# A two-block layer on one Trainium2 core: where the layer norm's sums stand in the order, who squares the MLP's tiles, and at what pace the mixers run

## What is computed

```python
# first block: 12 heads are mixed (4 gated linear attention, 4 HGRN, 4 cross attention)
proj = einsum('bsd,de->bse', rms_norm(x, norm_w), w_in)
gla_o  = merge_heads(rms_norm(chunked_gated_linear_attention(gq, gk, gv, gla_log_a), gla_norm_w))
hgrn_o = merge_heads(rms_norm(chunked_gated_linear_attention(hq, hgrn_k, hi, hgrn_log_f), hgrn_norm_w))
x = x + einsum('bse,ed->bsd', concatenate([gla_o, hgrn_o, xo]) * silu(gate), w_out)

# second block: conformer convolution, then the MLP
u = h @ w_pw1 + b_pw1
a, gate = split(u, 2)
u = dwconv(a * sigmoid(gate), w_dw) + b_dw          # 31 taps per channel
u = silu(layer_norm(u, ln_g, ln_b))                  # mean, then sum of squares, over the channels
xl = xl + g1 * (u @ w_pw2 + b_pw2)
xl = xl + g2 * (square(relu(modulate(rms_norm(xl)) @ w1)) @ w2)      # 4096 hidden
return rms_norm(xl, final_g)
```

## Time and profile before

| | |
|---|---|
| median of 3 runs | 2219.56 us (2217.82 to 2226.28) |
| the profiled execution | 2225.21 us, span 2223.4 us |
| TensorE's granted clock over the span | 0.961 of full speed |
| PE busy | 2099.5 us, 94% |
| DVE, ACT, POOL busy | 50%, 33%, 37% |
| products L1228 with WH, with WL | 951.7 us (x2976), 572.9 us (x1488) |

### The profile page before, as it was taken

The page is one execution under the profiler, slowest core; times in us unless marked ns, Lnnn a source line. Parts: engine busy times, 40 slices in busy tenths (PEclk is TensorE's granted clock), DMA queues, the critical chain, the costliest instruction groups (busy, mean ns, idle before and its releaser), DMA issues. The chain is left out here.

```text
span 2223.4 us, 26465 instructions
## 1 busy us (share of the span) xinstructions
PE 2099.5 (94%) x10318; PEld 1750.1 (79%) x10318; DVE 1120.0 (50%) x1941; ACT 723.1 (33%) x1251; POOL 825.6 (37%) x493
## 2 busy tenths in 40 slices
PE   7899999898998889999989988799999999999997
PEld 5778988787887678888878777667878888888886
DVE  5353455356463245455569968887425222222225
ACT  2312322211036622231456547442423222212211
POOL 7352122212111354443338857553344442222220
PEclk9999999999899999999999979899899999999998
DMA  4111011111001476776335422122223331111112
GB/s 161 58 57 52 16 58 57 39 34 34 29 29 39 144 292 227 236 242 212 114 135 190 180 79 80 59 74 76 76 77 101 98 95 57 59 55 48 48 48 76
DMA packets 68845, 213.55 MB, mean 96 GB/s; under 512 B 7648, under 2 KB 8032, under 8 KB 68592
## 3 DMA queue, kind: packets, MB, share of 16 engines
q1 hardware_dynamic: 54896, 186.69, 24.8%
q10 hardware_dynamic: 13824, 25.17, 3.6%
HBM read 182.47 MB, written 29.36 MB: 95 GB/s over the span
## 5 line engine op out<-in xcount | busy, mean ns | idle before, releaser
L1228 PE MATMUL B<-HB,WH 128*128 128x512 f32 x2976 | 951.7, 408 | 25.2 <-ACT WH L1625 11.0
L2457 POOL TENSOR_TENSOR WL<-RAW,WH 128x1024 fp32r<-128x1024 f32 x201 | 487.5, 2428 | 627.6 <-ACT WH L1625 623.5
L1228 PEld LDWEIGHTS B<-HB,WH 128*128 128x128 f32 x2976 | 562.2, 194 | 148.9 <-issue 28.0
L1228 PE MATMUL B<-HB,WL 128*128 128x512 f32 x1488 | 572.9, 399 | 7.6 <-POOL WL L2457 7.6
L1228 PEld LDWEIGHTS B<-HB,WL 128*128 128x128 f32 x1488 | 287.2, 193 | 73.0 <-POOL WL L2457 10.6
L1625 ACT ACTIVATE WH<-RAW 128x1024 fp32r<-128x1024 f32 x160 | 168.5, 1055 | 435.3 <-DMA RAW<-wall 421.6
L1939 DVE SCALAR_TENSOR_TENSOR B<-UP,vec,B 128x512 f32<-128x512 f32 x308 | 207.5, 746 | 0.0
L1939 DVE SCALAR_TENSOR_TENSOR RES<-B,modv,RES 128x512 f32<-128x512 f32 x144 | 104.5, 746 | 193.4 <-PE B L1411 167.6
L1411 PE MATMUL B<-HIDH,WH 128*128 128x512 f32 x512 | 188.4, 401 | 3.9 <-DVE RES L1939 2.0
L2434 POOL TENSOR_TENSOR small<-small 128x4 f32<-128x4 f32 (+2 forms) x36 | 36.7, 1019 | 397.1 <-DVE small L1942 397.0
L1411 PE MATMUL B<-HIDH,WL 128*128 128x512 f32 x512 | 183.6, 392 | 0.0
(11 more groups left out here) (242 smaller groups left out, 2733.2 us busy)
## 6 DMA issues: line engine op xcount, KB each, us to landing
RAW<-wall SPq DMA_DIRECT2D x201, 512.0 KB, 3.6
MODRAW<-wmod ACTq DMA_DIRECT2D x96, 256.0 KB, 4.3
WH<-parts SPq DMA_DIRECT2D x32, 512.0 KB, 3.2
WL<-parts SPq DMA_DIRECT2D x32, 512.0 KB, 4.2
RES<-xT SPq DMA_DIRECT2D x16, 512.0 KB, 8.9
oscr<-OT SPq DMA_DIRECT2D x32, 256.0 KB, 2.0
OI<-oscr SPq DMA_DIRECT2D x16, 512.0 KB, 5.2
parts<-WH SPq DMA_DIRECT2D x16, 512.0 KB, 5.2
```

The lines of the kernel that those rows point to most:

```text
L1228: i = pe.matmul(bank, a[:, ks], hb(part, k, h), start=k == 0 and n == 0, stop=k == 7 and n == 2)
L2457: po.tensor_tensor(lo, raw, hi.bitcast(F32), ALU.subtract).then_inc(sig[f"w_lo{q % NW}"], 1)
```

## The change

1. **The layer norm's sums.** `LATE` becomes 8 us for the first half and 22 for the second. Each `ysum` waits until 5 (first half) or 12 us (second half) after its `ysub` on the plan's clock, singly and no longer in pairs; `ln_row` until 5 us after `ln_r`. When all DVE channels of a half are out, the tap lanes' lead falls from 2.5 to -2.5 us, until the norm is written.
2. **The square.** ScalarE does Relu, Square (into the PSUM bank) and the high part; VectorE does only the low part. Two taps are put between in VectorE's order, where there are some.
3. **The MLP's order.** The first half's group 3 comes before the second half's pw2, and the hidden tiles 16 to 19 of the first half run beside the second half's norm. Their weights are loaded once per half, four units of 512 KB more.
4. **The mixers' pace.** Each step of a mixer has its own price in credit (0.6 to 1.5, before 1.0 for all). At the end of a q product only the mixer's own list is run out; what finishes a mixer stays for later products.
5. **The last levels.** The matmuls of levels 4 and 5 take 112 and 96 weight columns, not 128, and the masked copies as many partitions.

```diff
-LATE = 8.0
+LATE, LATE_SQ, LATE_ROW = (8.0, 22.0), (5.0, 12.0), 5.0
...
             elif h:
-                mlp[h] += [("w1", (g + 1) * GT + i, 2) for i in range(GT)]
+                mlp[h] += [("w1", (g + 1) * GT + i, h) for i in range(GT)]
...
         while credit[0] >= 1.0 and (bg or bg2):
-            credit[0] -= 1.0
-            step()
+            credit[0] -= step()
...
+    def mixed_up_to(n):
+        while len(bg) > n:
+            step_in(bg)
...
-            project(("gq", h), "q_out", h, lambda: drain(1))
+            project(("gq", h), "q_out", h, lambda: mixed_up_to(1))
...
-            project(("hq", n - 4), "q_out", n, lambda: drain(1 if i == 0 else 0))
+            project(("hq", n - 4), "q_out", n, lambda: mixed_up_to(1 - i))
...
+        if all((i, h) in co_done or i in BY_POOL[h] for i in range(8)):
+            ahead[0] = -2.5
...
     def normed(h):
         take(S, "ysum", h)
+        made = []
         for f in range(8):
             piece("ysub", f, h)
             piece("ysq", f, h)
-            if f % 4 == 3:
-                yield
+            made.append(now["dve"])
         for f in range(8):
+            yield from until(made[f] + LATE_SQ[h])
             piece("ysum", f, h)
             if f % 2:
                 yield
         piece("ln_r", h)
-        for _ in range(8):
-            yield
+        yield from until(now["pe"] + LATE_ROW)
...
+    def squared(i, h):
+        piece("hid", i, h)
+        for _ in range(2):
+            if lanes["dve"]:
+                lane_step("dve")
+        piece("hid_lo", i, h)
...
+    half_group(AHEAD_GROUPS - 1, 0)
...
     second_product(1)
     bg.append(before_mlp(1))
-    half_group(AHEAD_GROUPS - 1, 0)
+    for i in range(GT):
+        hidden(AHEAD_GROUPS * GT + i, 0)
     drain()
...
-                m = 64 if l == 6 else 128
+                m = 128 - (1 << l) if l > 3 else 128
...
                 ac.activation(RL[:, :], BANKS[b], ACT.Relu).then_inc(sig["hid_relu"], 1)
+                w.wait_ge(sig["hid_relu"], n)
+                ac.activation(BANKS[b], RL[:, :], ACT.Square).then_inc(sig["hid_sq"], 1)
...
-                stt(BANKS[b], BANKS[b], 0.0, RL[:, :], ALU.max, ALU.mult).then_inc(sig["hid_sq"], 1)
```

More of the change, by code:

```diff
@@ L37 @@
 COST = {"dve": {"glu": 0.7, "tap": 0.67, "taps_end": 0.7, "ysub": 0.7, "ln_r": 0.8, "z_mul": 0.7, "z_lo": 1.2, "pre": 0.75,
-                "pw2": 0.75, "sq_add": 0.65, "sq_add3": 0.7, "m1_mul": 0.66, "m1_lo": 0.66, "m2_mul": 0.75, "m2_lo": 1.5, "hid": 1.4,
+                "pw2": 0.75, "sq_add": 0.65, "sq_add3": 0.7, "m1_mul": 0.66, "m1_lo": 0.66, "m2_mul": 0.75, "m2_lo": 1.5, "hid_lo": 0.7,
                 "w2_out": 0.75},
@@ L86, in unit_plan @@
             elif h:
-                mlp[h] += [("w1", (g + 1) * GT + i, 2) for i in range(GT)]
+                mlp[h] += [("w1", (g + 1) * GT + i, h) for i in range(GT)]
             mlp[h] += [("w2", g, j, h) for j in range(4)]
-    plan += [("pw2", f, 0) for f in range(8)] + mlp[0][:-4]
-    plan += [("pw2", f, 1) for f in range(8)] + mlp[0][-4:] + mlp[1]
+    plan += [("pw2", f, 0) for f in range(8)] + mlp[0]
+    plan += [("pw2", f, 1) for f in range(8)] + [("w1", AHEAD_GROUPS * GT + i, 0) for i in range(GT)] + mlp[1]
     for g in range(AHEAD_GROUPS, HG):
@@ L258, in step @@
         turn[0] += 1
-        step_in(bg2 if (bg2 and turn[0] % 2) or not bg else bg)
+        return step_in(bg2 if (bg2 and turn[0] % 2) or not bg else bg)
     def step_in(lane):
         try:
-            next(lane[0])
+            return next(lane[0]) or 1.0
         except StopIteration:
             lane.pop(0)
+            return 1.0
+    def mixed_up_to(n):
+        while len(bg) > n:
+            step_in(bg)
     def drain(upto=0):
@@ L370, in finish @@
         for _ in range(LATER[0]):
-            yield
+            yield 0.6
         piece("scale", n, hh)
         for _ in range(LATER[1]):
-            yield
+            yield 0.6
         for f in range(tiles):
@@ L499, in make_plan @@
     for h in range(4):
-        project(("xq", h), "q_out", 8 + h, lambda: drain(1))
+        project(("xq", h), "q_out", 8 + h, lambda: mixed_up_to(1))
         bg.append(cross(8 + h))
-    while len(bg) > 1:
-        step()
+    mixed_up_to(1)
     ring = [G]
@@ L721, in means @@
         while left:
-            ready = [f for f in left if (f, h) in co_done and (now["pe"] > co_done[f, h] + LATE or hurry[0])]
+            ready = [f for f in left if (f, h) in co_done and (now["pe"] > co_done[f, h] + LATE[h] or hurry[0])]
             if ready:
@@ L728, in means, with until @@
             yield
+    def until(us):
+        while now["pe"] < us and not hurry[0]:
+            yield
     def normed(h):
         take(S, "ysum", h)
+        made = []
         for f in range(8):
@@ L757, in conv_norm @@
         yield from normed(h)
+        ahead[0] = AHEAD
     hi_by[0] = "act"
@@ L847, in hidden @@
         for h in halves:
-            piece("hid", i, h)
+            squared(i, h)
     def half_group(g, h):
@@ L888, in make_plan @@
         for i in range(GT):
-            hidden((g + 1) * GT + i, *((1,) if g + 1 < AHEAD_GROUPS else (0, 1)))
+            hidden((g + 1) * GT + i, 1)
         half_group(g, 1)
```

22 lines of the change are left out of this document (10 added, 12 removed).

## The result

| | before | with the change |
|---|---|---|
| median of 4 runs | 2218.69 us (2210.6 to 2226.28) | 2192.28 us (2187.83 to 2194.9) |
| profiled execution, span | 2225.21 us, 2223.4 us | 2192.47 us, 2190.7 us |
| mean granted clock | 0.961 | 0.971 |

The ratio is 0.9879, 95% interval 0.9841 to 0.9918: 26 us faster, where 40 were forecast. To see where they came from I cut both traces at five matmuls that stand in each kernel: the first of the gate (GLR,gupt), the last of the values (WL,HB, into B), the first with w_out (MXH,WH), the first mean (CO,ones), and the first MLP product with w2 (HIDH,WL). The last column ends at the last norm's first broadcast (FIN,ones). Each number is the time between two such matmuls, in us.

What follows compares the result with a forecast made beforehand. The prediction took TensorE, busy 94% of the span, as the bound, with gains only in its waits and half-clock stretches. Terms 13 + 6 + 3 + 1 + 9 + 7 + 1 = 40 us took 2219.6 to 2180, range 2152 to 2204.

Steps and rivals of the forecast that it cites:

- Mixers, the transposes: Transposes at mixer drains: waits for OSB and the half clock behind them go; 13 us, bounds 0 and 14.8.
- Levels of head 6: Head 6's mixer levels: a product step before each wait cuts idle time and half clock; 6 us, bounds 0 and 10.7.
- Mixers, the rest: Two more mixer transposes stand behind more products, less a cost for bare levels; 3 us, bounds -1.3 and 4.3.
- The rival that the mixers' gain is given back: Mixers: VectorE paces levels and chunks, waits return at later buffer uses, 22 us lost; 2202 us, chance 0.13.
- Narrower levels: Mixers' last levels: fewer weight columns shorten weight loads; 1 us, bounds 0 and 3.6.
- First half's layer norm: First half's sums of squares: the 7.81 us wait goes, most half clock stays; 9 us, bounds -1 and 23.3.
- Second half and hidden tiles: Second half: waits for mean and squares go, HIDL waits halve, 7 us; half clock at the sums, 1 us.
- The square: MLP hidden tiles: 64 squares moved to ScalarE run beside products, relieving VectorE; 0 us on the path.
- The rival that ScalarE becomes the path: MLP: each hidden tile waits for its square, 40 us come back; 2220 us, no change, chance 0.03.
- Extra units: MLP weights: four more loads and splits are covered by idle DMA, ScalarE and GpSimd; 0 us.
- The clock stayed up: Rival: full clock in both halves' sums, adding 14 us in the first and 11 in the second; 2155, chance 0.12.
- The slower rival: Mixer drains: longer runs without products lower the clock in each of six, 8.35 us apiece; 2235 us, chance 0.04.

Runs made afterwards that it cites:

- experiment 1: The kernel before, with only the change's placement of the first half's sums: 2201.71 us, ratio 0.9916.
- experiment 2: The changed kernel with the mixers' old pace and drains: 2187.66 us, ratio 0.9865.
- experiment 10: The changed kernel with the mixers' old pace, and the second half's sums of squares all single, each with a product step behind: 2189.52 us, ratio 0.9875.
- experiment 9: The changed kernel with the old pace and drains for the cross attention's heads 8 to 11 only: 2184.3 us, ratio 0.9845.
- experiment 6: The changed kernel with ScalarE making the first half's first square thirteen times, so PE waits before the first sum: 2207.99 us, ratio 0.9956.
- experiment 5: The changed kernel with the first half's eight sums in a row, no product step between: 2195.71 us, ratio 0.99.
- Experiment 8: The changed kernel with the second half's means and sums placed as before, the new MLP order kept: 2195.18 us, ratio 0.9899.
- experiment 3: The changed kernel with the MLP's square back on VectorE: 2194.64 us, ratio 0.9882.
- experiment 7: The changed kernel with the weights' high part in the mixers' stage on ScalarE, not GpSimd: 2196.92 us, ratio 0.9903.

## Why the prediction was right, and where it was wrong

The direction and the range held: 2192.28 lies between 2152 and 2204, and nearer to the slower end. The forecast of 2180 was 12 us too low, and that it is no further off is luck in part: the mixers' 23 us were all but lost, and the layer norms and the MLP gave some 14 more than forecast in the profiles. With the mixers' loss alone the time would have been at the edge of the range. The forecast's own range, 2163 to 2197, does not follow from its two bounds either: 13 and 10 us less gain make 2203.

- **Mixers, the transposes: 13 forecast, some 11 in their stage.** The two stalls did go, and in part the lower bound came, "the wait moves to another place". The wait of 4.02 us is one of the sort named as a sign of being wrong, though for set1k and not for OSB or set0k. A level now stands behind the forget gate in VectorE's queue (4.02 us, then 5 us at 0.53). The stage of heads 0 to 5 gained 10.8 us in the profile; in the five other profiles that have the whole new pace up to head 7 and GpSimd's split as it was it is 503 to 505 us, against 514 to 516 in the four of the old pace (before and experiments 1, 2 and 10).
- **Levels of head 6: 6 forecast, no gain found.** The step that failed is "a step (0.68) stands in front of each wait": the splits fall at another moment, VectorE's long steps lie elsewhere (577.6 us for 2.59, 581.8 for 2.05), and waits of 1.38 and 1.95 us follow. The clock falls as before. Over the profiles of either order the stretch is 7 to 27 us with the old pace and 14 to 24 with the new, so neither a gain nor a loss by the clock is shown.
- **Mixers, the rest: 3 forecast, lost.** The step that failed is "they now stand behind more products": the transposes that read OSB wait 10.1 us in this stage, before 8.0, and PE's idle time in it is 27 to 29 us, before 22 to 23; experiment 9 points to the cross attention's pace for the idle time. Heads 6 to 11 as a whole took 233.3 us for 223.8 in this pair of profiles, 227 to 233 for 218 to 227 over all. The rival that the mixers' gain is given back is what happened, and experiment 2 shows it in the time.
- **Narrower levels: 1 forecast, not measured.** No run has them alone, so their effect stays open. The weight loads became shorter by less than the width: 214 ns at 128 columns, 209 at 112 and 187 at 96, in means over both clock levels.
- **First half's layer norm: 9 forecast, 17.4 measured.** The two moves that take the wait away were read rightly: PE reached the first sum at 1296.4 and its square was there. The step that failed is "I expect most of this to stay", that the clock would be at the half in the sums whatever stood ahead. It stayed at 1.00, and experiment 6 shows that the wait decided. The mistake was to set rows against the wait that have one too: 1.7 us stood ahead of the earlier trace rows, with the sums in pairs behind it, and in the earlier trace rows, said to show a fall without idle time, PE was idle for 2.5 of the 6.6 us before it. That a fall can come with no wait at all is true, but it is seen only in experiment 5 and behind the pair of the second half, at sums without products between. The z chain then bounds the rest, as forecast: pw2 still waits 4.4 us.
- **Second half and hidden tiles: 7 and 1 forecast, 13.5 for the last stage.** The mean's wait and the squares' wait went, as said. The half of the HIDL waits did not: they are 5.4 us for 3.8. What was underpriced is "For the half clock at these sums I take 1": the low stretch went from 23.7 to 13.7 us, worth 5 by the clock. Experiment 8 puts 6 to 11 us of the stage down to the sums.
- **The square: 0 forecast, open.** By the time nothing, by the last stage of experiment 3 a gain of 3 to 9 us. ScalarE's price was right:

```profile
L1931 ACT ACTIVATE B<-RL 128x512 f32<-128x512 f32 x16 | 9.6, 603 | 0.5
```

603 ns, against 622 taken. The rule of the Trainium skill's page "ScalarE: Activation LUTs" (section Rules for kernel authors) puts multiplies on VectorE, but gives the factor of three for bf16 with one source; the prediction left this condition out. This float32 tile falls outside it: VectorE's multiply took 692 ns, and taking it back made the waits longer. The rival that ScalarE becomes the path did not come.
- **Extra units: 0 forecast, 0 found.** Among PE's waits behind 1360 none is for WL.
- **Rivals.** The clock stayed up in the first half (half of that rival). There the section HAM oscillation of the Trainium skill's page "TensorE: Matmul & The Clock Gate", that waits between stretches of work are to blame, agrees with experiment 6; experiment 5 has a fall with no wait, which that section doesn't cover. The slower rival didn't come: the half clock in head 6's levels is within what the old order shows.

## What to carry to other kernels

A wait of PE in front of thin work is to be priced with the clock behind it: here 6.4 us of wait cost 13.6 more by the clock, and 16 in the time. When a stall at a drain is removed by leaving the work for later, look which step then stands behind which in the queue of the engine that feeds it; here the transposes' 5.56 and 5.43 us became one wait of 4.02 at a level. With several parts in a change, a table of stages between matmuls that all kernels share tells them apart where the total does not; but it takes several profiles of an order, since one stage differed by 6 us among them.

## What was not expected of the hardware

- The same alternation of one-column sums and product steps ran wholly at 1.00 (1296 to 1315 in the changed kernel) and at 0.50 (1296.8 to 1324 in experiment 6), by whether a wait of 6.40 us stood ahead of it. PE was busy almost all the time in both.
- Eight sums in a row lowered the clock with no idle time ahead, and it was back three product steps later (experiment 5).
- A multiply of VectorE with both inputs in SBUF, 0.41 us alone, took 2.56 while GpSimd split a weight unit (experiment 7), and a step with one tensor input took 2.83 for 0.81 (the changed kernel). The Trainium skill's page "GPSIMD Engine Reference" (section Specifications) says that the two share SBUF interfaces, with contention for instructions of two SBUF inputs or in a two-port mode. The rows agree for two inputs; whether the step with one input ran in such a mode no row shows.
